# One table value a tile, register branches, scatter ahead of gather, and the last norm inside the experts' block

## The reference

```python
def hier_moe(h, ...):                       # h: 2048 tokens x 1024
    group  = argmax(h @ router_wg + bg)     # 4 groups
    top_v, top_i = top_k(expert logits of that group, 2)
    gate = softmax(top_v) * group probability
    for e in range(16):
        hid = silu(xt @ exp_w1[e]) * (xt @ exp_w3[e])   # 1024 -> 256
        y  += gate[:, e] * (hid @ exp_w2[e])            # 256 -> 1024
h = layer_norm(ALPHA * h + ffn, ln2_g, ln2_b)
```

## Time and profile before

| | us |
|---|---|
| median of 3 runs (lowest, highest) | 1588.07 (1587.83, 1590.92) |
| profiled execution | 1591.52 |
| its span | 1589.8 |
| TensorE busy in the span | 1444.7 (91%) |
| VectorE, ScalarE, GpSimd busy | 1129.6, 928.1, 487.5 |

### The profile page before, as it was taken

One profiled execution on the slowest core, in us unless ns is written; L12 is line 12 of the kernel. 1 busy time (PEld: TensorE's weight loads), 2 busy tenths in 40 slices (PEclk: granted clock), 3 DMA queues, 4 the chain that ended last, 5 costly groups with the idle time before them and its releaser, 6 DMA issues. The chain is left out here.

```text
span 1589.8 us, 30237 instructions
## 1 busy us (share of the span) xinstructions
PE 1444.7 (91%) x8945; PEld 1256.8 (79%) x8947; DVE 1129.6 (71%) x2198; ACT 928.1 (58%) x1626; POOL 487.5 (31%) x348
## 2 busy tenths in 40 slices
PE   5999999999997999999999999965999999999940
PEld 5999977777766999999999999953877887887820
DVE  8787558999987888888888888877454334444237
ACT  4444348787887666666666666633555445555325
POOL 1212124465531011112111111121455433555318
PEclk9999999999998999999999999986999999999965
DMA  8865642444452121111212111146797787786576
GB/s 291 305 228 193 231 149 99 180 146 172 162 187 74 57 85 60 60 60 60 96 66 79 60 60 60 47 147 228 212 287 205 219 231 186 217 270 149 110 226 260
DMA packets 125382, 246.95 MB, mean 155 GB/s; under 512 B 24434, under 2 KB 77682, under 8 KB 125300
## 3 DMA queue, kind: packets, MB, share of 16 engines
q1 hardware_dynamic: 93168, 157.82, 28.9%
q0 software_dynamic: 12528, 45.99, 12.6%
q10 hardware_dynamic: 19604, 42.09, 7.0%
HBM read 151.20 MB, written 94.67 MB: 155 GB/s over the span
## 5 line engine op out<-in xcount | busy, mean ns | idle before, releaser
L1807 DVE TENSOR_TENSOR d_probs_t_lo<-d_pt_ps,d_probs_t_hi 128x512 fp32r<-128x512 f32 x256 | 164.9, 686 | 69.3 <-ACT d_probs_t_hi L1722 68.1
L1722 ACT ACTIVATE d_probs_t_hi<-d_pt_ps 128x512 fp32r<-128x512 f32 x256 | 139.3, 596 | 98.7 <-PE d_pt_ps L1602 92.2
L1788 DVE TENSOR_REDUCE d_neg_max<-d_s_ps 128x1 f32<-128x1024 f32 x128 | 155.3, 1214 | 0.2 <-PE d_s_ps L1591 0.2
L124 PE MATMUL e_a_ps<-up_hi,e_xt_hi 128*128 x336 | 138.9, 414 | 12.2 <-issue 8.3
L124 PE MATMUL acc<-k_hi,wl_hi 128*128 128x256 f32 x512 | 144.5, 282 | 4.5 <-DVE k_lo L619 4.5
L1705 ACT ACTIVATE d_probs<-d_s_ps,d_neg_max 128x1024 f32<-128x1024 f32 x128 | 143.4, 1120 | 0.9 <-DVE d_neg_max L1788 0.9
L126 PE MATMUL acc<-k_hi,wl_lo 128*128 128x256 f32 x512 | 143.7, 281 | 0.0
L125 PE MATMUL acc<-k_lo,wl_hi 128*128 128x256 f32 x512 | 143.6, 280 | 0.0
L1602 PE MATMUL d_pt_ps<-ident,d_probs 128*128 128x128 f32 x1024 | 133.7, 274 | 4.6 <-ACT d_probs L1705 4.6
L125 PE MATMUL e_a_ps<-up_lo,e_xt_hi 128*128 x336 | 134.7, 401 | 0.0
L126 PE MATMUL e_a_ps<-up_hi,e_xt_lo 128*128 x336 | 133.8, 398 | 0.0
(11 more groups left out here) (443 smaller groups left out, 4152.1 us busy)
## 6 DMA issues: line engine op xcount, KB each, us to landing
up_raw<-in_exp_w SPq DMA_DIRECT2D x32, 1024.0 KB, 7.5
down_raw<-in_exp_w SPq DMA_DIRECT2D x16, 1024.0 KB, 14.4
d_h_tile<-h_dram SPq DMA_DIRECT2D x16, 522.0 KB, 4.8
h_dram<-v_all ACTq DMA_DIRECT2D x16, 512.0 KB, 3.3
ht_hi_dram<-k_hi ACTq DMA_DIRECT2D x8, 1024.0 KB, 4.3
ht_lo_dram<-k_lo ACTq DMA_DIRECT2D x8, 1024.0 KB, 6.7
q_tile<-q_dram SPq DMA_DIRECT2D x16, 512.0 KB, 4.1
q_dram<-wq_raw ACTq DMA_DIRECT2D x15, 512.0 KB, 3.4
```

The costliest lines, as they stand in the source:

```text
L124: pe.matmul(out, lhs[0], rhs[0], start=first, stop=False)
L1722: act.activation(pt_hi[:, c * HALF:(c + 1) * HALF, h % 2], pt_ps[c][:], ACT.Copy).then_inc(pth_done[c], 1)
L1788: dve.tensor_reduce(nm[:, u, h:h + 1], s_ps[h % 2][:], AX, ALU.max, negate=True).then_inc(nm_done, 1)
L1807: dve.tensor_tensor(pt_lo[:, part, h % 2], pt_ps[c][:], pt_hi[:, part, h % 2].bitcast(F32), ALU.subtract)\
```

## The change

**Tables.** `split_at` and `pair_live` are gone. `split_next` holds, for each tile, the number of the expert whose weights are to be split beside it, or 0; it is loaded once a tile and kept in a register for both splits. A pair's branch compares the register that holds the last tile's number. `before_last` is last_tile - 1, used once at the end.

**Order within a tile.** TensorE's `turn_hid(j)` moves to the start of `up(j+1)`, behind the branch and the load of the expert's number. VectorE's wait for the scatter and the two copies move from the end of tile j to tile j+1, behind `hid` (`keep`). GpSimd's scatter of tile j-1 stands ahead of the gather of tile j+3. In the route, its wait for the index lists is the last of its three.

**SyncE.** `w_ready` for expert e+1 is signalled before the wait for the low parts of e.

**Last norm.** `combine` becomes `last_norm`, whose parts run in the experts' block, behind each engine's own last tile. Constants, the rows of gain and bias and their broadcast don't wait for the rows any more. All sixteen row tiles are loaded at one place. Moments are taken tile by tile and interleaved with other work, ScalarE takes the sums of six tiles (8 to 11, 14, 15), VectorE does six tiles whole, GpSimd multiplies by the gain in four, and the last store is in two halves.

```diff
-        def beside_first_tile(eng, j, split):
-            flag = eng.value_load(split_at[0:1, bass.ds(j, 1)], min_val=0, max_val=1)
-            with eng.If(flag > 0):
-                split(eng.value_load(tile_expert[0:1, bass.ds(j, 1)], min_val=0, max_val=NE - 2) + 1)
+        def to_split(eng, j):
+            return eng.value_load(split_next[0:1, bass.ds(j, 1)], min_val=0, max_val=NE - 1)
...
                 begin(j, u)
+                e = to_split(eng, j) if split_first or split_rest else None
                 if split_first:
-                    beside_first_tile(eng, j, split_first)
+                    with eng.If(e > 0):
+                        split_first(e)
                 up(j, u)
+                if keep and not is_first:
+                    keep(j - 1, 1 - u)
                 turn(j + 1, 1 - u)
-                ahead(j + 3, 1 - u)
                 if not is_first:
                     down(j - 1, 1 - u)
+                ahead(j + 3, 1 - u)
                 turn_hid(j, u)
                 if split_rest:
-                    beside_first_tile(eng, j, split_rest)
+                    with eng.If(e > 0):
+                        split_rest(e)
...
             def pair(n, then=None):
-                flag = eng.value_load(pair_live[0:1, bass.ds(n, 1)], min_val=0, max_val=1)
-                with eng.If(flag > 0):
+                with eng.If(last > 2 * n):
...
             with sp.Fori(0, NE // 2 - 1) as n:
                 for b in range(2):
-                    sp.wait_ge(w_in[b], 48 * n + 48)
+                    sp.wait_ge(w_in[1 - b], 48 * (n + b) + 48)
                     sp.sem_inc(w_ready, 1)
                     for made, parts in lo_parts:
                         sp.wait_ge(made, parts * (2 * n + b + 1))
...
             def up(j, u):
                 e = expert_of(pe, j)
+                if not (isinstance(j, int) and j < 1):
+                    turn_hid(j - 1, 1 - u)
...
-            run_tiles(pe, skip, skip, None, up, turn, down, turn_hid, None, down_with)
+            last = run_tiles(pe, skip, skip, None, up, turn, down, skip, None, last_down)
+            norm_pe(pe, last)
...
                 dve.tensor_tensor(ht_lo[:], h_ps[:], ht_hi[:].bitcast(F32), ALU.subtract).then_inc(hl_done, 1)
-                need(dve, y_added, 16 * (j - 1))
+
+            def keep(j, u, landed=None):
+                need(dve, y_added, 16 * (j - 1 if landed is None else landed))
                 dve.nop(nofuse=True)
                 dve.tensor_copy(gate[u][:], own_gate[u][:])
...
+def last_norm(nc, sem, ln_g, ln_b, sum_dram, out, x, x_in, rows, wide, ended, sb, ps):
+    POOL_GAIN = (0, 1, 2, 4)
+    DVE_ALL = (3, 6, 9, 11, 14, 15)
+    ACT_SUMS = (3, 5)
+    def on_pe(pe, last):
+        pe.wait_ge(consts, 2)
+        pe.wait_ge(rows_in, 32)
+        for n, (row, taken, behind) in enumerate(((g_row, xl_done, 3), (b_row, yt_done, 2))):
+            for half, cols in enumerate(HALVES):
+                pe.wait_ge(taken[half], last + behind)
+                pe.matmul(wide[n][:, cols], ones[:], row[:, cols], start=True, stop=True).then_inc(spread, 1)
+    def on_dve(dve):    # its order
+        moments(0) moments(1) moments(2) norm(0) moments(3) moments(4) norm(1) moments(5) moments(6) moments(7)
+        whole(3) moments(12) norm(2) moments(13) whole(6) norm(4) gain(5) gain(7) gain(12) gain(13) norm(3)
+        whole(9) gain(8) gain(10) whole(11) norm(5) whole(14) whole(15, HALVES)
+    def on_act(act):    # its order
+        [broadcast rows to SBUF] take_root(0) normalise(0) normalise(1) take_root(1) normalise(2) sums(8) sums(9)
+        take_root(2) sums(10) normalise(4) normalise(5) take_root(4) normalise(7) sums(11) normalise(12)
+        normalise(13) take_root(3) sums(14) normalise(8) normalise(10) sums(15) take_root(5)
```

More of the change, by code:

```diff
@@ L76 @@
 NEWTON = 3
-EARLY = 6
 EARLY_W = 6
@@ L2008, in load_expert, with route @@
     sp.dma_start(down_raw[:, b], part(exp_w2)).then_inc(loaded, 16)
[L2011 removed]
+def route(nc, sem, logits, lists, tile_expert, split_next, before_last, last_tile, h1_dram, sum_dram,
           exp_w1, exp_w3, exp_w2, up_w, down_w, last_rows, h1_stored, ix, xg, gathered, room, banks,
@@ new lines, in on_dve @@
+        dve.memset(ones[:], 1.0).then_inc(consts, 1)
+        dve.memset(eps[:], LN_EPS / ALPHA ** 2).then_inc(consts, 1)
+        moments(0)
+        moments(1)
+        moments(2)
+        norm(0)
+        moments(3)
+        moments(4)
+        norm(1)
+        moments(5)
+        moments(6)
+        moments(7)
+        whole(3)
+        moments(12)
+        norm(2)
+        moments(13)
+        whole(6)
+        norm(4)
+        for t in (5, 7, 12, 13):
+            gain(t)
+        norm(3)
@@ new lines, in on_dve, with take_root, sums, normalise @@
+        whole(9)
+        gain(8)
+        gain(10)
+        whole(11)
+        norm(5)
+        whole(14)
+        whole(15, HALVES)
+    def on_act(act):
+        def take_root(g):
+            j, n = NORMS.index(g) % 2, SIZES[g]
+            if g in ACT_SUMS:
+                act.wait_ge(sums_done, SUMMED.index(FIRSTS[g]) + n)
+                act.activation(root[g][:, 0:n], spread_sum[g][:, 0:n], ACT.Sqrt, bias=eps[:], scale=1.0 / D)\
+                   .then_inc(root_done, 1)
+                return
+            act.wait_ge(mv_done, FROM_STATS.index(g) + 1)
+            act.activation(root[g][:, 0:n], mv[j][:, 0:n, 1], ACT.Sqrt, bias=eps[:]).then_inc(root_done, 1)
+        def sums(t):
+            (g, i), n = place(t), SUMMED.index(t)
+            act.wait_ge(x_in[t], 16)
+            if n:
+                act.wait_ge(sums_done, n)
+            act.activation(junk, x[t], ACT.Copy, accum_out=total[g][:, i:i + 1]).then_inc(total_done, 1)
+            act.wait_ge(total_done, n + 1)
+            act.activation(less_mean[g][:, i:i + 1], total[g][:, i:i + 1], ACT.Copy, scale=-1.0 / D).then_inc(mean_done, 1)
+            act.wait_ge(mean_done, n + 1)
+            act.activation(junk, x[t], ACT.Square, bias=less_mean[g][:, i:i + 1],
+                           accum_out=spread_sum[g][:, i:i + 1]).then_inc(sums_done, 1)
+        def normalise(t):
+            g, i = place(t)
+            act.wait_ge(ln_done, NORMS.index(g) + 1)
+            act.activation(x[t], x[t], ACT.Identity, bias=shift[g][:, i:i + 1], scale=rstd[g][:, i:i + 1])\
+               .then_inc(xn_done, 1)
+        act.wait_ge(consts, 2)
+        act.activation(warm[:], eps[:], ACT.Sqrt)
+        for n, kept in enumerate((g_b, b_b)):
+            for half, cols in enumerate(HALVES):
+                act.wait_ge(spread, 2 * n + half + 1)
+                act.activation(kept[:, cols], wide[n][:, cols], ACT.Copy).then_inc(kept_done, 1)
+        take_root(0)
+        normalise(0)
+        normalise(1)
+        take_root(1)
+        normalise(2)
+        sums(8)
+        sums(9)
+        take_root(2)
+        sums(10)
+        normalise(4)
+        normalise(5)
+        take_root(4)
+        normalise(7)
+        sums(11)
+        normalise(12)
+        normalise(13)
+        take_root(3)
+        sums(14)
+        normalise(8)
+        normalise(10)
+        sums(15)
+        take_root(5)
```

424 lines of the change are left out of this document (177 added, 247 removed).

## The result

The changed kernel takes 1563.12 us, median of 4 runs (1561.77 to 1564.39), against 1587.95 us (1587.61 to 1590.92) for the kernel before on the same chip: a ratio of 0.9835, 95% interval 0.9811 to 0.986. The forecast was 1562, range 1556 to 1575. The profiled execution took 1562.47 us, its span 1560.5, which is 29.3 us shorter than before's; the medians differ by 24.8. Timed a second time, the same kernel gave 1564.23 (5 runs, 1563.09 to 1566.23) against 1588.62.

What follows compares the result with a forecast made beforehand. TensorE was taken to bound the experts' loop, VectorE's list of work the last norm. Loop -18, start -5.5, tail -1.2 and norm -4.6 sum to -29.3, from 1591.5 to 1562 us; range 1556 to 1575.

Steps and rivals of the forecast that it cites:

- Loop: Forty tiles of the experts' loop: 18 of 19.6 us lost near weight-splitting tiles would go; ends 6 and 19.6.
- SyncE's new wait cost nothing: Experts' loop: SyncE's new wait for a weights' load, issued at least two tiles earlier, was costed at nothing.
- Order of scatter and gather: Loop's tail: with the scatter ahead, it is issued 0.3 us earlier and lands 0.9 sooner; -1.2 (0 to -2).
- The collision: Experts' loop: one VectorE low part lost 5.0 us beside GpSimd's subtractions, within the 19.6; staying had chance 0.08.
- VectorE should be first: Weight splits: VectorE's down part comes about 1.5 us earlier, GpSimd's about 1 us, so VectorE gets the shared port.
- the collision moves to another split tile: Rival, experts' loop: port conflict stays or moves, 5.0 us plus some 2 at the lower clock; 1569 us, chance 0.08.
- Start: Before tile 1: TensorE loses about 3.1 us of idle time, regains 2.4 of clock; -5.5, ends -2 and -6.
- Last norm: Final norm: VectorE ends 4.4 us earlier and the halved last store gives 0.2; -4.6, ends 0 and -7.9.
- Slower rival: Experts' loop: scatters landing after 9.6 us or more use up the gain; at 10.8, about 1640 us; chance 0.03.

Runs made afterwards that it cites:

- ready only: Kernel before with one edit: SyncE signals the weights of expert e+1 before waiting for the low parts of e; 1581.69 us, ratio 0.9952.
- loop-only kernel: Kernel before with every change of tables, branches and order, but the old last norm in its own block; 1569.5 us, ratio 0.9873.

## Why the prediction was right, step by step

**Loop (-18; measured -19.6).** Right in mechanism: ScalarE's earlier high parts, an earlier hid, and loads out of the way of TensorE's wait. The runs show that the parts overlap. Undone one at a time in the changed kernel, they cost 2.1 (loads), 0.6 (hid), 2.8 (scatter wait), 4.1 (SyncE's signal) and 4.1 us (order of scatter and gather), middles of the two differences; done alone in the kernel before, hid's move brought 7.9, the same edit. One reading of the forecast was off: in tile 33 the transposes began at 1435.49, not near 1435.7, so hid was there at +3.5, not +3.3, against a need at +3.6. And tile 25 of before, 4.3 us over a quiet one without any collision (TensorE waited 1.62 us for hid itself, at 1350.43), had no term of its own. A late hid costs what stands behind the wait for it, and any edit that brings hid in time takes that away from all others. The size of a load was 0.57, not 0.45 us, on the favourable side. "SyncE's new wait cost nothing" held: no tile waits for it.

**Order of scatter and gather.** The forecast counted it in the tail only, -1.2 us. This is the step that failed: the tail gave 0.15. The row behind it, 0.48 us of "issue" at 1518.76, was read as a delay by the gather, but the scaled y was there no sooner; in the changed kernel GpSimd waits for it for 6.47 us and issues at the same distance from the transposes. The last scatter followed 7.2 instead of 7.4 us later. The swap's worth is in the loop: it keeps the gather between the scatter's issue and the subtractions, and with the loads gone that is what keeps VectorE out of the collision: in the changed kernel the subtraction follows the issue at 2.9 us or more.

**The collision.** Forecast: 5.0 us of the 19.6, about 7 if it stays, and "VectorE should be first". The outcome is right, no long part in two profiles. The price is not: 5.6 us of VectorE's time cost 1.03 us a tile with the gather first, and 1.3 in the kernel with the loads gone (about 1.8 with what followed). Tile 8 of before, 5.07 us over a quiet one, holds more than the collision, as TensorE's rows in it show:

```profile
1180.98 0.44 PE L2538 MATMUL e_h_ps<-ident,e_hid 128*128 128x128 f32 x2 [1.01 <-DVE e_hid L2647]
...
1183.45 0.49 PE L124 MATMUL e_a_ps<-up_hi,e_xt_hi 128*128 x1 [2.03 <-issue]
...
1190.64 1.03 PE L2516 MATMUL e_t_ps<-ident,xg 128*128 128x128 f32 x8
```

Besides the late hid there are 2.03 us of "issue", which hid's place in TensorE's stream added, and an up pass of 7.2 us instead of 5.6. And the reason for being first was half wrong. Not arrival alone decides. In ten cases of two kernels GpSimd's subtraction followed the start of the scatter's issue by 1.05 us, VectorE had begun 0.36 to 0.58 us behind that start, 0.47 to 0.69 us before the subtraction, and it lost every time. At the same distance it won once, when it began 0.70 us behind the issue (ready only, 1130.09). Where the distance was 1.13 us or more, VectorE took 1.2 us, except in the case in which GpSimd's subtraction was 20 ns ahead of it. With the loads in the kernel the distance was 1.13 us or more in all such splits but that one; without them and without the swap it was 1.05 in all five long ones. What inside GpSimd makes the difference is not shown. So the rival "the collision moves to another split tile" was nearer than its 0.08: without the swap it happens five times, for 5 us in all.

The Trainium skill ("SBUF — State Buffer", "SBUF: two separate sides") has an exclusive lock: the engine that starts first holds the pair for the whole instruction, and the other fully blocks. A wait for whole instructions agrees with 6.87 us, ending 1.1 us behind the second subtraction. That the first to start gets it does not agree: in all ten cases VectorE's row starts before GpSimd's subtraction. That GpSimd takes the port with its issue and keeps it from one instruction to the next would fit these rows, but no run shows it.

**Start (-5.5; measured -5.0).** Composition as forecast. The route with its longer chain of table work came 0.48 us later in this profile (1094.26 against 1093.78), of the size of its spread between kernels. The run with SyncE's old order shows 5.2 us to be that edit's alone.

**Last norm (-4.6; measured -4.5).** VectorE's list 41.61 instead of 42.14 us (-0.5; forecast -0.9), its start 1.1 earlier (forecast 1.1), idle time 2.9 instead of 5.9 (forecast 3.4), the last store 0.15 (forecast 0.2). The loop-only kernel confirms 4.5 us from the other side.

**Slower rival.** The scatter chain: GpSimd waits for the previous scatter's landing, but landing stayed at 7 us and no tile is longer for it.

**The number.** The sum was held against the profiled execution, which ran 3.6 us over the median of before's runs (3.4 over the three known then), while the changed kernel's profiled one ran 0.7 under its own. So the medians differ by 24.8 us, not 29.3. Taken from the median of before, the same sum would have said 1558.8; that 1562 came within 1.1 us of 1563.12 is in part luck. The 5.1 us of tile 8, counted both in the 18 and in the 19.6, stood in the one profile of before; whether its other runs had them is not known.

## What to carry to other kernels

Where an engine runs dry behind "issue", look at what stands behind its last wait: moving one wait below two loads brought 8 us alone, and nearly nothing once the data came early. Don't price a part by undoing it in the finished kernel only; where several edits serve one deadline, each looks cheap. When loads or waits are taken out of an engine that shares a memory port, see which of its instructions now follow each other more closely: the saving can hand the other engine a wait that it didn't have.

## What the hardware showed that I had not expected

A subtraction of GpSimd that follows its own DMA issue closely can keep VectorE out although VectorE began first: 10 of the 11 times that VectorE began between the issue and a subtraction 1.05 us behind it, and never at 1.13 or more. It goes the other way as well. In the changed kernel's start, VectorE's low parts run back to back from 1098.19 to 1104.0, and GpSimd's gather issue within them took 3.44 us instead of 0.98:

```profile
1100.52 3.49 DVE L2393 TENSOR_TENSOR up_lo<-up_raw,up_hi  x3
...
1101.38 3.44 POOL L2489 DMA_INDIRECT xg<-h_dram,ix  x1 [9.95 <-DVE ix L2647]
```

A register load from a table with its register work and branch cost ScalarE 0.57 us, of which the load itself is 0.28.
